# Gate chain without POOL's middle steps, query projection in halves, and output gate units among the last head's work

## What is computed

```
q, v, zf, zb, g = jnp.split(h @ w_in, N_HG_PROJ, axis=-1)
...
log_f = jnp.logaddexp(jnp.log(lb), jnp.log1p(-lb) + jax.nn.log_sigmoid(z))
k = (1.0 - lb) * jax.nn.sigmoid(-z)
...
cum = jnp.cumsum(log_f, axis=3)
ref = cum[:, :, :, HG_CHUNK // 2 - 1:HG_CHUNK // 2, :]
scores = jnp.einsum('bhnck,bhnsk->bhncs', q * jnp.exp(cum - ref), k * jnp.exp(ref - cum))
...
chunk_kv = jnp.einsum('bhnck,bhncv->nbhkv', k * jnp.exp(last - cum), v)
...
inter = jnp.einsum('bhnck,nbhkv->bhncv', q * jnp.exp(cum), s_prev)
return (intra + inter).reshape(b, h, l, dv), s_final
```

## Time and profile before

| | |
|---|---|
| median of three runs | 2893.68 us (2891.71 to 2897.15) |
| the profiled execution's own time | 2899.64 us |
| its span in the profile | 2897.8 us |
| busy share of the span: PE, DVE, ACT, POOL | 75%, 38%, 28%, 10% |
| turn 0 of the head loop begins on PE | 169.94 us |
| turn 14, turn 15 | 518.33 us, 538.54 us |
| output projection begins | 614.74 us |

### The profile page before, as it was taken

The page is one execution under the profiler, slowest core; times in us unless marked ns, Lnnn a source line. Parts: engine busy times, 40 slices in busy tenths (PEclk is TensorE's granted clock), DMA queues, the critical chain, the costliest instruction groups (busy, mean ns, idle before and its releaser), DMA issues. The chain is left out here.

```text
span 2897.8 us, 41688 instructions
## 1 busy us (share of the span) xinstructions
PE 2162.8 (75%) x17466; PEld 1521.8 (53%) x17466; DVE 1111.6 (38%) x1676; ACT 818.9 (28%) x1349; POOL 278.0 (10%) x268
## 2 busy tenths in 40 slices
PE   5988989696998399676667553899988676766652
PEld 4866666596776288533323222677766532333221
DVE  3277777734322444520011105666545520111103
ACT  4166666422222522310100104433323310100101
POOL 2022222201100100100000001111101100000001
PEclk8999999796999699788888776999988788888876
DMA  8365655245884422599999993211112599999995
GB/s 315 113 205 195 201 199 187 70 102 191 314 318 175 153 93 83 218 395 410 396 413 412 404 395 129 70 45 45 45 45 74 218 364 409 405 408 413 408 411 196
DMA packets 218830, 698.38 MB, mean 241 GB/s; under 512 B 24365, under 2 KB 123382, under 8 KB 161782
## 3 DMA queue, kind: packets, MB, share of 16 engines
q1 hardware_dynamic: 195446, 625.04, 57.4%
q0 software_dynamic: 12992, 33.10, 3.3%
q10 hardware_dynamic: 10176, 37.23, 3.2%
HBM read 664.34 MB, written 45.11 MB: 245 GB/s over the span
## 5 line engine op out<-in xcount | busy, mean ns | idle before, releaser
L220 PE MATMUL PS<-ring,arena 128*32 128x256 f32 (+5 forms) x7488 | 805.2, 492 | 403.3 <-DMA ring<-in_moe_w_up 166.1
L220 PE MATMUL PS<-second 128*128 128x256 f32 (+1 forms) x4416 | 812.5, 343 | 57.9 <-DVE second L239 28.4
L220 PEld LDWEIGHTS PS<-ring,arena 128*32 128x32 f32 (+3 forms) x7488 | 418.3, 140 | 751.5 <-issue 592.6
L220 PEld LDWEIGHTS PS<-second 128*128 128x128 f32 x4416 | 680.7, 196 | 165.1 <-ACT arena L232 30.0
L232 ACT ACTIVATE arena<-PS 128x512 f32<-128x512 f32 (+1 forms) x346 | 171.6, 496 | 1069.4 <-PE PS L220 896.2
L239 DVE TENSOR_TENSOR arena<-arena,PS 128x256 f32<-128x256 f32 (+1 forms) x83 | 43.5, 524 | 748.5 <-PE PS L220 747.6
L220 PE MATMUL PS<-arena 128*64 128x64 f32 (+8 forms) x1600 | 275.3, 365 | 27.1 <-DVE arena L239 12.8
L228 PE MATMUL PS<-ident,arena 128*128 128x128 f32 x919 | 140.4, 302 | 157.6 <-ACT arena L232 92.6
L232 ACT ACTIVATE arena<-arena 128x512 f32<-128x512 f32 (+5 forms) x255 | 182.5, 716 | 258.9 <-DVE arena L239 124.4
L258 DVE COPY arena<-PS 128x512 f32<-128x512 f32 (+4 forms) x169 | 93.6, 554 | 413.6 <-PE PS L220 371.4
L220 PEld LDWEIGHTS PS<-arena 128*128 128x128 f32 (+5 forms) x1600 | 161.2, 174 | 144.3 <-issue 113.7
(11 more groups left out here) (157 smaller groups left out, 1118.0 us busy)
## 6 DMA issues: line engine op xcount, KB each, us to landing
ring<-in_moe_w_up SPq DMA_DIRECT2D x148, 1024.0 KB, 12.5
ring<-in_moe_w_down SPq DMA_DIRECT2D x148, 1024.0 KB, 11.3
ring<-in_moe_w_gate SPq DMA_DIRECT2D x142, 1024.0 KB, 11.4
ring<-in_ada_w SPq DMA_DIRECT2D x48, 1024.0 KB, 5.5
y_d<-arena ACTq DMA_DIRECT2D x51, 512.0 KB, 8.3
ring<-in_w_mod SPq DMA_DIRECT2D x24, 1024.0 KB, 6.7
ring<-in_gdn_in_w SPq DMA_DIRECT2D x32, 512.0 KB, 4.1
ring<-in_hg_w_in SPq DMA_DIRECT2D x24, 512.0 KB, 6.9
```

Of the source, the lines that this page charges most:

```text
L220: return P.e.matmul(o, l, r, start=st, stop=sp)
```

## The change

1. The elementwise round: DVE clips with a minimum (negative values) and subtracts; "y" becomes one tensor_scalar (add, max) in place of two; ACT's second Abs reads "sp" with a bias and no longer waits for "y". POOL keeps only "t3", which now waits for "y"; "x4", qt and the second part of cx go to DVE. The Exps and products stand in another order.
2. PE's turn: the query projection is cut into two halves of 12 matmuls, the first at the end of the even turn, the second near the start of the odd one. The states stand behind one half of "zl" and a modulation piece, "z" ahead of the outputs. `MODS_OF` begins with piece 13, so that one piece stands ahead of turn 0 where there were four, and the fourth piece of a turn, with two transposes, stands at the turn's end.
3. DVE and ACT: the round's first two parts run ahead of the evictions; the sum of outputs of turn it-1 stands in turn it, ahead of the masked scores; the query's split stands on its own.
4. The output gate: unit 0's first half runs in turn 15 between scores and states, its second behind the loop, with no meeting on PE; the row product moves behind unit 2. Unit 0 is loaded and split a turn earlier, and unit 1's split stands in turn 15.

```diff
-    for n in range(16, 72):
-        MODS_OF[(n - 16) // 4].append(n)
+    for n in range(13, 72):
+        MODS_OF[(n - 13) // 4].append(n)
...
+    def q_pe(h, half):
+        b = bank("q", h) if half else take(state["q"], "q", h)
...
+        for k in range(4 * half, 4 * half + 4):
...
@@ hgrn_pe
-        mods_pe(range(12, 16))
+        mods_pe((12,))
         for it in range(16):
             Z = proj_pe(it + 2) if it < 14 else iter(())
             ms = MODS_OF[it]
             scores_pe(it)
-            next(Z, None)
+            if it == 15:
+                mod_turn_pe(17, state["body"])
+                state["banks"][3] = ("ev", "mod", 17)
+                state["all"] = banks(*ALL)
+                gated_half_pe(hg2, "g", 0, 0, state["all"], latent)
             mods_pe(ms[0:1])
-            if it == 14:
-                mod_turn_pe(17, state["body"])
-            states_pe(it)
+            if it % 2 and it < 14:
+                q_pe((it + 1) // 2, 1)
             next(Z, None)
             mods_pe(ms[1:2])
-            outputs_pe(it)
+            states_pe(it)
             next(Z, None)
             mods_pe(ms[2:3])
             next(Z, None)
+            outputs_pe(it)
+            if it % 2 == 0 and it < 14:
+                q_pe(it // 2 + 1, 0)
             mods_pe(ms[3:4])
+        P.end("hgrn")
@@ elem_ac
-        A.wait_ge(at("y", it))
-        act(T[1], T[4], ACT.Abs, "ya", it)
+        A.wait_ge(at("sp", it))
+        act(T[1], T[2], ACT.Abs, bias=nd[:, c:c + 1])
@@ hgrn_ac
             next(E, None)
-            if it and it % 2:
+            next(E, None)
+            if it % 2:
                 output_ac(it - 1)
             turned_ac(it)
             next(E, None)
...
+            if MODS_OF[it]:
+                mod_ac(MODS_OF[it][2])
             if it < 13:
-                splits_ac(it + 3)
+                split_ac((it + 3) % 2, it + 3, 5)
@@ elem_ve
-        tt(T[2], T[2], T[1], ALU.add, "sp", it)
+        tt(T[2], T[2], T[1], ALU.subtract, "sp", it)
         V.wait_ge(at("ge", it - 1) if it else at("zz"))
-        ts(T[4], T[2], -1.0, nd[:, c:c + 1], ALU.mult, ALU.add, "y", it)
-        V.wait_ge(at("ya", it))
-        ts(T[4], T[4], 0.0, la[:, c:c + 1], ALU.max, ALU.add)
+        ts(T[4], T[2], lbm[:, c:c + 1], la[:, c:c + 1], ALU.add, ALU.max, "y", it)
@@ hgrn_ve
             E = elem_ve(it + 1) if it < 15 else iter(())
             next(E, None)
+            next(E, None)
             turned_ve(it)
+            if 1 <= it < 15:
+                mod_ve(it + 2)
+            if it:
+                output_ve(it - 1)
+            scores_ve(it)
+            if it % 2 == 0 and 2 <= it <= 12:
+                split_ve("q", it + 2, 7)
             next(E, None)
-            scores_ve(it)
             states_ve(it)
+            if it == 15:
+                mod_ve(17)
+                low("g", 1)
+            next(E, None)
...
-            next(E, None)
-            next(E, None)
-            output_ve(it)
-            if it < 13:
-                splits_ve(it + 3)
-            if it == 15:
                 low("g", 0)
+        output_ve(15)
@@ elem_gp
+        G.wait_ge(at("y", it), at("ev", "zl", it), G.here())
+        gtt(T[3], T[0], T[2], ALU.subtract, "t3", it)
@@ gate_pe
-        P.end("hgrn")
-        meet(P, "hgrn")
-        turn = state["all"] = banks(*ALL)
-        row_pe(view(10240, F), "g1row", turn)
-        for u in range(4):
-            gated_pe(hg2, "g", u, turn, lambda k: (at("hg2hi", k), at("hg2lo", k)))
-            if u:
-                turn_gated_pe(u - 1, turn)
+        gated_half_pe(hg2, "g", 0, 1, turn, latent)
+        for u in range(1, 4):
+            gated_pe(hg2, "g", u, turn, latent)
+            if u == 2:
+                row_pe(view(10240, F), "g1row", turn)
+                turn_gated_pe(0, turn)
+                turn_gated_pe(1, turn)
+        turn_gated_pe(2, turn)
         turn_gated_pe(3, turn)
```

More of the change, by code:

```diff
@@ L679, in hgrn_sp @@
         ahead_sp(1)
-        for n in range(12, 16):
-            mod_sp(n, turn)
+        mod_sp(12, turn)
         for it in range(16):
-            if it == 15:
+            if it == 14:
                 state["slots"].update({s_: ("ps", "z", 15) for s_ in (1, 2, 3)})
@@ L715, in proj_pe @@
         yield
[L716 to L720 removed]
+    def q_pe(h, half):
+        b = bank("q", h) if half else take(state["q"], "q", h)
+        hi, lo = h2p[7]
+        P.wait_ge(at("hi", "hq", h), at("lo", "hq", h))
+        for k in range(4 * half, 4 * half + 4):
+            P.wait_ge(at("hg2hi", k), at("hg2lo", k))
+            i = mm3(b, (hi[:, k, :], lo[:, k, :]), (hg2[0][:, k, :], hg2[1][:, k, :]), k == 0, k == 7)
+        if half:
+            i.then_inc(*P.mark("ps", "q", h))
     def scores_pe(it):
@@ L771, in hgrn_pe @@
             pass
+        for half in range(2):
+            q_pe(0, half)
         for _ in proj_pe(1):
             pass
-        mods_pe(range(12, 16))
+        mods_pe((12,))
         for it in range(16):
@@ L836, in elem_ac @@
         yield
+        A.wait_ge(at("cum", it))
+        act(T[2][:, 0:512], T[5][:, 256:768], ACT.Exp, "e4", it)
         A.wait_ge(at("x0", it))
@@ L839, in elem_ac @@
         act(T[0][:, 0:512], T[0][:, 0:512], ACT.Exp, "e2", it, scale=-1.0)
-        act(T[2][:, 0:512], T[5][:, 256:768], ACT.Exp, "e4", it)
+        A.wait_ge(at("x4", it))
+        act(T[4], T[4], ACT.Exp, "e3", it)
         A.wait_ge(at("x5", it))
@@ L845, in elem_ac @@
         act(dec[i], tiles(T[5])[:, :, 127 if d == 0 else 0], ACT.Exp, "dec", it)
-        A.wait_ge(at("x4", it))
-        act(T[4], T[4], ACT.Exp, "e3", it)
         yield
@@ L878, in hgrn_ac @@
             next(E, None)
-            if it and MODS_OF[it - 1]:
-                mod_ac(MODS_OF[it - 1][3])
             if it == 15:
-                state["pairs"]["turn"] = Turn((0, 1), {0: ("ps", "z", 15), 1: ("ps", "z", 15)})
-                high(("ps", "g", 0, 1), "g", 0)
-            next(E, None)
+                high(("ps", "g", 1, 1), "g", 1)
             next(E, None)
@@ L887, in hgrn_ac @@
                 squares_ac(it - 1)
+            if it % 2 and it < 13:
+                split_ac("q", it + 3, 7)
             next(E, None)
+            if it == 14:
+                state["pairs"]["turn"] = Turn((1, 0), {0: ("ps", "mod", 71), 1: ("ps", "z", 15)})
+                high(("ps", "g", 0, 1), "g", 0)
+            if MODS_OF[it]:
+                mod_ac(MODS_OF[it][2])
             if it < 13:
-                splits_ac(it + 3)
+                split_ac((it + 3) % 2, it + 3, 5)
         squares_ac(15)
@@ L1031, in hgrn_gp @@
         for it in range(16):
-            for _ in elem_gp(it):
-                pass
+            elem_gp(it)
     def transposed2_pe(src, name, turn, *before):
@@ L1080, in row_ac, with gated_half_pe, gated_pe @@
             act(dst[:, n * 512:(n + 1) * 512], bank(name, n), ACT.Copy, "ev", name, n)
-    def gated_pe(a, name, u, turn, made):
+    latent = lambda k: (at("hg2hi", k), at("hg2lo", k))
+    def gated_half_pe(a, name, u, p, turn, made):
         hi, lo = pair(name, u)
         P.wait_ge(at("hi", name, u), at("lo", name, u))
-        for p in range(2):
-            b = take(turn, name, u, p)
-            for t in (2 * p, 2 * p + 1):
-                c = slice(t * 128, (t + 1) * 128)
-                for k in range(8):
-                    P.wait_ge(*made(k))
-                    i = mm3(b[:, (t % 2) * 256:(t % 2) * 256 + 256], (a[0][:, k, c], a[1][:, k, c]), (hi[:, k, :], lo[:, k, :]), k == 0, k == 7)
-            i.then_inc(*P.mark("ps", name, u, p))
+        b = take(turn, name, u, p)
+        for t in (2 * p, 2 * p + 1):
+            c = slice(t * 128, (t + 1) * 128)
+            for k in range(8):
+                P.wait_ge(*made(k))
+                i = mm3(b[:, (t % 2) * 256:(t % 2) * 256 + 256], (a[0][:, k, c], a[1][:, k, c]), (hi[:, k, :], lo[:, k, :]), k == 0, k == 7)
+        i.then_inc(*P.mark("ps", name, u, p))
+    def gated_pe(a, name, u, turn, made):
+        for p in range(2):
+            gated_half_pe(a, name, u, p, turn, made)
     def two(b):
```

62 lines of the change are left out of this document (20 added, 42 removed).

## The result

| | before | after |
|---|---|---|
| median of five runs | 2893.68 us (2891.71 to 2904.0) | 2877.22 us (2872.89 to 2877.46) |
| ratio | | 0.9937 (0.992 to 0.9955) |
| the profiled execution's own time | 2899.64 us | 2872.89 us |
| its span | 2897.8 us | 2871.0 us |

On another chip, beside the experiments, the same kernel came to a ratio of 0.9915 (0.9893 to 0.9937). So the change is faster, by 0.6 to 0.9%, 16 to 26 us by the medians. The forecast was 41.9 us less, 2851.8 us, with a range from 2834 to 2874: the sign held, the size did not, and the time lies 3 us above the range.

What follows compares the result with a forecast made beforehand. The prediction took the loop to be bound by the elementwise round, coupled to PE. Terms of -11.5, -14.0, -3.2 and -13.2 us total -41.9, taking the 2893.68 us median to 2851.8, range 2834 to 2874.

Steps and rivals of the forecast that it cites:

- What bounds the loop: Head loop after the change: even turns stall 3.7 us for a PSUM bank, plus 2.0 slow matmuls; pair 47.6 us, -14.0 in all.
- Rival A: Head loop: the stall comes but the clock holds; pair 45.6, 2839.8 us; chance 0.2 together with no stall at all.
- the 2.0 us for the clock: Head loop, each pair of turns: slow matmuls behind the stall cost 2.0 us, with bounds of nothing and 2.4 us.
- The price at nothing: Head loop: POOL's remaining operation beside the copy of the turned keys costs 0, with bounds of 0 and 1.85 us.
- rival B: Head loop: POOL's operation blocks the copy, even turns +1.9, pair 49.5, 2863.2 us; chance 0.23.
- Up to turn 2: From the start to turn 2: turn 2 begins at 207.2 instead of 218.71, -11.5 us.
- the first round can end at about 161.5: Ahead of turn 0: the first elementwise round can end at about 161.5 us; PE had begun at 169.94.
- Turn 14 to 15: End of the head loop: 17.0 us instead of 20.2, -3.2, with three modulation pieces in PE's idle time.
- From turn 15 to the output projection: Turn 15 and the output gate: 63.0 us instead of 76.2, -13.2.
- Behind the output projection at nothing: Everything behind the output gate stage is moved whole, at a change of 0.
- cases of the loop: Head loop: stall with slow matmuls (0.5), the first part of Rival A and most of rival B, which the range takes.

Runs made afterwards that it cites:

- e3: Changed kernel with the modulation's two transposes moved into the next turn, behind its second modulation piece; ratio to the kernel before 0.9768.
- e4: Changed kernel with DVE adding the last turn's output before it copies the turned keys and adds the modulation vector; ratio to the kernel before 0.9842.
- e7: e6 plus ACT's unit 2 silus ahead of the row product's and first transposes' copies, last three modulation loads ahead of the first gate load; ratio to before 0.9733.
- e6: Changed kernel with the edits of e1 and e3 together; ratio to the kernel before 0.9755.
- e1: Changed kernel with the split of the output projection's first unit one gate unit later on ACT and DVE; ratio to the kernel before 0.9865.
- e2: Changed kernel with POOL's three scattered stores issued only after the output projection's first unit has been loaded; ratio to the kernel before 0.9903.

## Why the prediction was right or wrong

- **What bounds the loop: right.** The wait that takes the place of the two old ones is where it was forecast, ahead of the 64-column matmuls of every even turn from 2, put down to DVE, none ahead of the transposes. 3.79 us against 3.7, slow matmuls 2.5 against 2.0, own work 41.4 (e3) against 41.9, pair 47.7 against 47.6. e3 shows the bank as the cause: with another holder before the scores the wait is gone. Rival A (no slow clock) did not come in the changed kernel; in e4, with a wait 0.93 us shorter, it came in three of seven turns. That the 2.0 us for the clock, a mean of six other waits, came so near the 2.5 is in part luck, since nothing in the working said which way the clock would go.
- **The price at nothing: right, by more than the absence of a wait.** In the changed kernel's timelines of POOL and DVE the copy from PSUM and the sum of outputs both run under POOL's instruction at the duration they have alone, so rival B is out:

```profile
355.12 1.81 POOL L266 TENSOR_TENSOR arena<-arena 128x768 f32<-128x768 f32 x1 [21.65 <-DVE arena L246]
```

```profile
354.36 0.68 DVE L246 TENSOR_SCALAR arena<-arena,lbc 128x768 f32<-128x768 f32 x1
355.14 0.69 DVE L258 COPY arena<-PS 128x512 f32<-128x512 f32 x1
355.87 0.17 DVE L239 TENSOR_TENSOR mod<-PS,cols 128x8 f32<-128x8 f32 x1
356.07 0.69 DVE L239 TENSOR_TENSOR arena<-arena,PS 128x512 f32<-128x512 f32 x1
```

  The rule of the Trainium skill that stood beside it ("SBUF — State Buffer", "Who interferes with whom", at most one SBUF input, outside the two-port modes: no contention) agrees with both rows, 0.69 us each. Both read PSUM; that one SBUF operand is what matters, and not the kind of operation, is not told apart by these rows.
- **Up to turn 2: 2.0 us off.** The step "the first round can end at about 161.5" failed; turns 0 and 1 took 45.0 us, forecast 45.7. The round ended at 164.2. It began 1.6 us later than in the trace before (first clip at 148.68, before at 147.12), and took 15.5 us from there, only 0.7 less than before (16.2) where I had counted 1.8 less: its ten products and differences run without a gap for 7.04 us. The later start is PE's clock. The round begins behind the projections ahead of the loop, and in both traces these 120 matmuls of 512 columns begin at the same time (135.96 before, 135.91 after) behind the same wait of 2.81 us; they take 22.47 us before and 24.08 after, with a granted clock of 1.00 and 0.92 from 136 to 158. In the ten other runs, all edits of the changed kernel or itself, they take 24.1 to 25.3 us; whether that comes of the change or the one trace before was lucky, the runs don't tell. The forecast had taken the start over from the kernel before.
- **Turn 14 to 15: 1.4 us off.** I said that the modulation pieces moved here lie in PE's idle time. Their loads do not: PE waits 0.48, 0.56 and 1.67 us for them. With these loads issued ahead of the gate's (e7), one wait is left of the three that e6 has there.
- **From turn 15 to the output projection: the step that failed, 11.3 of the 15 us.** "I count: ... 3.5 units at 11.6 ... plus 1.0 slow", with "DVE's normalisation and the next split" as the only work of others that I asked about, and "Loads: the third unit's is issued about 18 us in, ahead of POOL's scattered stores". I checked the load of the next gate unit and DVE, but not what stands in ACT's queue ahead of the evictions that free PE's banks: the split of the first *output* unit, and the load behind that. It is the same kind of fault that I had found in the loop, a PSUM bank behind another engine's queue, one stage later. The change itself made it: the split had stood one unit later, behind unit 2's silus, and unit 3 had taken the banks of unit 1. I had read that unit 0 is split a turn earlier, and did not follow the other splits, which moved with it.

  By parts: turn 15 with the half unit took 14.1 us (514.06 to 528.17), 2.5 less than counted; from there on 60.2 us, 13.8 more, of which 9.17 are the wait, 2.3 the slow matmuls behind it (granted clock 0.50 from 573 to 577) and 1.49 a wait for DVE's split. e1 shows 6 to 7 us to be the order of ACT's queue. The 3 us that stay stand behind ACT's copies in the same queue; in e7, which moved these, PE doesn't wait there, though a gap of unknown cause within the unit takes the gain back. DVE's queue has no gap of over 0.2 us from 533.53 to the end of the split that PE waits 1.49 us for, and one of its tensor_tensors is 1.59 us longer beside POOL's product (last section): an estimate is that this is the whole of that wait, which no run tested. That the stores are what makes the load late is shown by e2.
- **Behind the output projection at nothing: right**, 0.5 us.
- **The range** left that stretch no room: it was made of cases of the loop, and the one stretch whose ops were all moved, and which had the second largest term, had no case of its own.

## What to carry to other kernels

When a change moves work of the bottleneck engine, or makes it earlier at some place, go through every engine that hands a buffer back to it there, and read its queue in the changed program from that hand-back upwards: each instruction that now stands ahead of it, and the load that this one waits for, is a candidate. A rotation of few buffers over many takers is sensitive to who takes one in between; moving two small transposes was worth more here (6.3 us a pair) than the three steps taken from POOL (nothing, as long as the bank was the bound). And a slow transfer moved out of one load's way has to be followed to the next load and to its own reader before it is called hidden.

## What the runs showed of the hardware

- **Scattered stores slow other queues' loads.** Three stores of 8 KB in 4-byte elements take 23 to 29 us, counted from the last issue to the fetch of their results, and a load of 1 MB from another queue beside them takes 22 to 25.5 us instead of 5.2. Stretches of 5 us of the changed kernel, the last three columns being granted clock, DMA share and GB/s:

```profile
553.00:558.00 5.00, 5.00 (x44) 5.00 (x44) 0.19 (x1) 0.00 (x0) 0.00 (x0) 1.00 0.82 26
558.00:563.00 5.00, 4.95 (x33) 3.70 (x31) 0.00 (x0) 1.29 (x3) 0.00 (x0) 1.00 0.85 37
```

  The DMA engines are 0.8 busy and move 26 to 37 GB/s. In e2 the load alone had this:

```profile
551.00:556.00 5.00, 5.00 (x42) 5.00 (x43) 4.56 (x5) 1.71 (x3) 0.00 (x0) 1.00 0.68 213
```

- **An idle time of PE costs more than itself, but not by its length alone.** In the changed kernel all seven waits of 2.70 to 4.07 us are followed by matmuls at the lower level of the clock; in e4, waits of 2.85 and 2.86 us are followed by slow scores in turns 2 and 4 and by nothing slow in turns 6 to 10, and the 3.13 us of turn 12 by matmuls that are slow only a microsecond later. Ahead of the loop the same wait of 2.81 us is followed by 22.47 us of matmuls at the full clock in the kernel before, and by 24.08 us for the same matmuls in the changed one. What else decides it, the runs don't tell.
- **A tensor_tensor with two operands from SBUF was held up beside POOL.** Of the tensor_tensors of `og` the one that begins beside POOL's product (533.60 to 536.5) takes 2.81 us and ends 1.1 us behind it, the next takes 1.22:

```profile
534.79 2.81 DVE L239 TENSOR_TENSOR arena<-arena,vec 128x1024 f32<-128x1024 f32 x1
537.64 1.22 DVE L239 TENSOR_TENSOR arena<-arena,small 128x1024 f32<-128x1024 f32 x1
```
